# A fifth value chunk multiplied behind the arriving modulation, and modulation halves spread anew, in a two-layer float32 kernel

## The reference

```python
m_l = silu(c) @ ada_w + ada_b                       # six rows of 2048
n_l = rmsnorm(h_lat, g) * (1 + m_l[1]) + m_l[0]
z = gelu(n_l @ w_in); u, v = split(z, 2)            # w_in: 2048 x 8192
v = rmsnorm(v, g_v); s = einsum('gpq,bnqgc->bnpgc', w_s, v) + b_s
h_lat = h_lat + m_l[2] * ((u * s) @ w_out)          # w_out: 4096 x 2048
n_l = rmsnorm(h_lat, g2) * (1 + m_l[4]) + m_l[3]
h_lat = h_lat + m_l[5] * conv_ffn(n_l, ...)         # 2048 -> 11264 -> 2048
```

## Time and profile before

| | before |
|---|---|
| median of 3 runs | 2331.35 us (2327.18 to 2331.69) |
| profiled execution, its own time | 2325.37 us |
| its span, mean granted clock | 2323.7 us, 0.992 |
| TensorE products | 2277.0 us busy, 98% |
| VectorE, ScalarE, GpSimd | 1573.1, 1134.1, 113.5 us |
| loaded | 488.49 MB, 211 GB/s over the span |

### The profile page before, as it was taken

One profiled execution on the slowest core, in us unless ns is written; L12 is line 12 of the kernel. 1 busy time (PEld: TensorE's weight loads), 2 busy tenths in 40 slices (PEclk: granted clock), 3 DMA queues, 4 the chain that ended last, 5 costly groups with the idle time before them and its releaser, 6 DMA issues.

```text
span 2323.7 us, 34580 instructions
## 1 busy us (share of the span) xinstructions
PE 2277.0 (98%) x13320; PEld 1990.9 (86%) x13320; DVE 1573.1 (68%) x2103; ACT 1134.1 (49%) x1698; POOL 113.5 (5%) x206
## 2 busy tenths in 40 slices
PE   6999999999999999999999999999999999999998
PEld 5788888888888888888888889999999999878887
DVE  6988777677788865666656677566566645555655
ACT  3354444444454543555445564444544444555554
POOL 0010100011100100000000001000000000100000
PEclk9999999999999999999999999999999999999999
DMA  9999788789767765555555565444444545544453
GB/s 368 387 369 394 239 283 266 243 314 316 263 217 254 280 205 184 187 176 199 193 187 182 185 199 168 159 150 141 146 146 145 163 150 164 163 135 126 132 185 126
DMA packets 230043, 493.06 MB, mean 212 GB/s; under 512 B 9683, under 2 KB 12521, under 8 KB 226825
## 3 DMA queue, kind: packets, MB, share of 16 engines
q1 hardware_dynamic: 210384, 432.05, 55.1%
q0 software_dynamic: 14272, 50.99, 6.7%
q10 hardware_dynamic: 5256, 8.20, 1.1%
HBM read 488.49 MB, written 2.10 MB: 211 GB/s over the span
## 4 chain that ended last, share of the span: by engine, by line
PE 85%; DVE 6%; DMA 3%; issue 3%; ACT 1%; SPq 1%; POOL 0%; DVEq 0%; ACTq 0%; POOLq 0%
PE ps L1846 35%; PE ps L1893 22%; PE ps L1908 11%; PE ps L1910 5%; PE ps L2363 4%; DVE acc L1195 2%; DMA mods<-in_ada_w 2%; DVE wlo L1129 1%; PE ps L2186 1%; DMA ada<-in_ada_w 1%; SPq L414 1%; DVE acc L1138 1%; PE ps L2348 1%; PE ps L2205 1%; PE ps L2004 1%
## 5 line engine op out<-in xcount | busy, mean ns | idle before, releaser
L1129 DVE TENSOR_TENSOR wlo<-raw,whi 128x1024 fp32r<-128x1024 f32 x720 | 874.2, 1223 | 532.1 <-ACT whi L587 530.7
L587 ACT ACTIVATE whi<-raw 128x1024 fp32r<-128x1024 f32 x720 | 756.2, 1057 | 821.0 <-PE ps L1846 398.7
L1908 PE MATMUL ps<-xt__59,whi 128*128 128x512 f32 x1408 | 499.1, 399 | 5.8 <-DVE wlo L1129 4.3
L1910 PE MATMUL ps<-xt__59,wlo 128*128 128x256 f32 x1408 | 395.5, 281 | 0.0
L1846 PE MATMUL ps<-whi,xt__59 128*128 128x512 f32 x1024 | 329.7, 399 | 4.2 <-DVE xt__59 L1247 4.2
L1908 PEld LDWEIGHTS ps<-xt__59,whi 128*128 128x128 f32 x1408 | 265.3, 188 | 73.8 <-DVE wlo L1129 5.6
L1893 PE MATMUL ps<-xmh__60,whi 128*128 128x272 f32 x1088 | 322.7, 297 | 0.6 <-DVE h L1326 0.3
L1893 PE MATMUL ps<-xmh__60,wlo 128*128 128x272 f32 x1088 | 314.9, 289 | 0.0
L1893 PE MATMUL ps<-xml__61,whi 128*128 128x272 f32 x1088 | 313.0, 288 | 0.0
L1910 PEld LDWEIGHTS ps<-xt__59,wlo 128*128 128x128 f32 x1408 | 266.5, 189 | 0.1
L1846 PEld LDWEIGHTS ps<-whi,xt__59 128*128 128x128 f32 x1024 | 195.6, 191 | 46.1 <-issue 4.5
(11 more groups left out here) (335 smaller groups left out, 3267.8 us busy)
## 6 DMA issues: line engine op xcount, KB each, us to landing
raw<-in_a_w_in SPq DMA_DIRECT2D x128, 1024.0 KB, 5.5
raw<-in_ffn_w_up SPq DMA_DIRECT2D x88, 1024.0 KB, 5.1
ada<-in_ada_w POOLq DMA_DIRECT2D x96, 512.0 KB, 4.4
raw<-in_a_w_out SPq DMA_DIRECT2D x48, 1024.0 KB, 5.3
raw<-in_ffn_w_down SPq DMA_DIRECT2D x44, 1024.0 KB, 5.1
mods<-in_ada_w SPq DMA_DIRECT2D x64, 512.0 KB, 11.1
raw<-in_b_w_in SPq DMA_DIRECT2D x32, 1024.0 KB, 5.4
ada<-in_ada_w SPq DMA_DIRECT2D x16, 1024.0 KB, 8.9
```

The source lines that it names most:

```text
L587: act.activation(whi[:, r % 4], raw[:, r // 2, r % 2], ACT.Copy).then_inc(hi_ready, 1)
L1129: dve.tensor_tensor(wlo[:, r % 4], raw[:, r // 2, r % 2], whi[:, r % 4].bitcast(F32), ALU.subtract).then_inc(lo_ready, 1)
L1908: pe.matmul(both, whi[:, r % 4, i, c * P:c * P + P], xt_[:, :, k * T:k * T + T], start=first and i == 0, stop=last and i == 1, skip_group_ ...
L1910: mm = pe.matmul(ps[:, bank + c, 0:T], wlo[:, r % 4, i, c * P:c * P + P], xth[:, k, :], start=False, stop=last and i == 1, skip_group_chec ...
```

## The change

- Group g of the front has ten units for five v chunks (`S_ORDER`, `S_UNITS`): chunk 4 goes through banks 6 and 7 as well, behind chunk 3 in the same group. Each group has five slabs. Chunks 5 to 7 (24 units) are left for behind.
- ScalarE copies the parts of chunks 3 and 4 of groups 0 to 2 into three buffers each. VectorE adds them in group 3 (`add_parts`, `add_last`), the last part straight from PSUM. GpSimd's `add3` is gone.
- Six low parts instead of four stand between the additions of the next group. `keep_warm` has 8 transposes for 14.
- The memsets of `acc` on GpSimd wait until the last low tile is done (`nl` at 16), and `stream_ada(3)` until ten value outputs are.
- The 16 loads of `ada2` and their additions are spread over 12 slabs and 24 units, in place of 16 and 32.
- `ADA4_AT` has more in the first output chunk and fewer in the last, `ADA5_OUT_AT` eight for two, `ADA5_AT` six for eight in a pair.

```diff
-S_CHUNKS = (3, 0, 1, 2)
-LATE_LO = (0, 1, 2, 4)
+S_ORDER = ((3, 0, 4, 1, 2),) * 3 + ((3, 0, 1, 2, 4),)
+LATE_LO = (0, 1, 2, 4, 4, 5)
+S_UNITS = 10
...
 def first_unit(u):
...
-    g, i, half = u // 8, u % 8 // 2, u % 2
-    return S_CHUNKS[i], 4 * g + 2 * half
+    g, i, half = u // S_UNITS, u % S_UNITS // 2, u % 2
+    return S_ORDER[g][i], 4 * g + 2 * half
...
 def mod_adds(g, d):
...
-ADA4_AT = [(0, t) for t in (9, 11, 13, 15)] + [(n, t) for n in (1, 2) for t in (0, 4, 5, 6, 8, 9, 10, 12, 13, 14)]\
-    + [(3, t) for t in (0, 1, 2, 4, 5, 6, 7, 8)]
-ADA5_OUT_AT = (12, 13)
+ADA4_AT = [(0, t) for t in (6, 8, 9, 10, 11, 13, 14, 15)] + [(n, t) for n in (1, 2) for t in (0, 4, 5, 6, 8, 9, 10, 12, 13, 14)]\
+    + [(3, t) for t in (0, 4, 5, 6)]
+ADA5_OUT_AT = (7, 8, 9, 10, 11, 12, 13, 14)
...
-ADA5_AT = (0, 1, 2, 6, 8, 9, 10, 14)
+ADA5_AT = (0, 2, 6, 8, 10, 14)
...
-        whole3 = place("whole3", [P, 2, 512], O_H)
-        part3 = place("part3", [P, 2, 512], O_H + 4 * KB)
+        part3 = [place(f"part3{i}", [P, 2, 512], x) for i, x in enumerate((O_H, O_H + 4 * KB, O_H + 12 * KB))]
+        part4 = [place(f"part4{i}", [P, 2, 512], x) for i, x in enumerate((O_ADA, O_ADA + 4 * KB, O_H + 8 * KB))]
...
                     for i in range(2):
...
-                for q, c in enumerate(S_CHUNKS):
-                    slab(G_IN + g, q, w_in, g, c * 512 + GW)
-            for k in range(16):
-                slab(G_IN + 4 + k // 4, k % 4, w_in, k % 4, k // 4 * 512 + (4 * 512 + GW))
-                if k >= 4:
-                    sp.wait_ge(mod_added, mod_adds(3, 7) + k - 3)
-                else:
-                    sp.wait_ge(mod_added, mod_adds(3, last_in_slot(k)))
-                sp.dma_start(ada2[:, k % 4], ada_w[k * P:k * P + P, 2 * D:3 * D]).then_inc(mod_loaded[k % 4], 16)
+                for i, c in enumerate(S_ORDER[g]):
+                    n = 5 * g + i
+                    slab(G_IN + n // 4, n % 4, w_in, g, c * 512 + GW)
+            k = 0
+            for n in range(12):
+                slab(G_IN + 5 + n // 4, n % 4, w_in, n % 4, n // 4 * 512 + (5 * 512 + GW))
+                while k < 16 * (n + 1) // 12:
+                    if k >= 4:
+                        sp.wait_ge(mod_added, mod_adds(3, 7) + k - 3)
+                    elif last_in_slot(k) in PE_MOD[3]:
+                        sp.wait_ge(mod_turned, mod_columns(3))
+                    else:
+                        sp.wait_ge(mod_added, mod_adds(3, last_in_slot(k)))
+                    sp.dma_start(ada2[:, k % 4], ada_w[k * P:k * P + P, 2 * D:3 * D]).then_inc(mod_loaded[k % 4], 16)
+                    k += 1
...
-            def add3(g):
-                pool.wait_ge(sem("part3_copied"), 2 * g + 2)
-                if g > 1:
-                    pool.wait_ge(sem("part3_added"), g - 1)
-                pool.tensor_tensor(whole3[:, :, :], whole3[:, :, :], part3[:, :, :], ALU.add).then_inc(sem("part3_added"), 1)
-            add3(1)
-            add3(2)
...
+            pool.wait_ge(sem("nl"), 16)
...
-            add3(3)
+            pool.wait_ge(sem("v_ready"), 10)
...
-            stream_ada(5, 32, 0, 2)
+            stream_ada(5, 32, 0, 5)
...
-            stream_ada(5, 32, 2)
+            stream_ada(5, 32, 5)
...
-            def part3_out(g):
-                act.wait_ge(unit_used, 8 * g + 2)
-                if g > 1:
-                    act.wait_ge(sem("part3_added"), g - 1)
+            def part_out(g, part, used):
+                act.wait_ge(unit_used, used)
                 for tok in range(2):
-                    act.activation((part3 if g else whole3)[:, tok], ps[:, 6 + tok, :], ACT.Copy)\
-                       .then_inc(sem("part3_copied"), 1)
-            def v_out(c, par, used=None):
-                if par is None:
-                    act.wait_ge(sem("part3_added"), 3)
-                else:
+                    act.activation(part[g][:, tok], ps[:, 6 + tok, :], ACT.Copy).then_inc(sem("part_copied"), 1)
+            def v_out(c, par, used=None, whole=None, added=0):
+                if added:
+                    act.wait_ge(sem("part_added"), added)
+                if whole is None:
...
                 for tok in range(2):
-                    src = whole3[:, tok:tok + 1, :] if par is None else ps[:, 2 * par + tok:2 * par + tok + 1, :]
+                    src = ps[:, 2 * par + tok:2 * par + tok + 1, :] if whole is None else whole[:, tok:tok + 1, :]
...
                 for r in range(8):
                     if r == 3:
                         if first:
-                            v_out(2, 2, 32)
+                            v_out(3, 0, whole=part3[0], added=3)
...
-                    if first and r == 6:
-                        v_out(3, None)
+                    if first and r == 5:
+                        v_out(4, 0, whole=part4[0], added=6)
...
                     if first and r == 1:
-                        v_out(1, 1, 30)
+                        v_out(2, 2, 38)
...
             def ws_load(c):
...
             for g in range(4):
-                for u in (8 * g, 8 * g + 1):
+                for u in (10 * g, 10 * g + 1):
...
-                for i in range(8):
-                    u = 8 * g + i
+                for i in range(10):
+                    u = 10 * g + i
+                    if g == 3 and i == 9:
+                        v_out(0, 0, 34, added=5)
                     if i > 1:
...
-                    if i == 5:
-                        part3_out(g)
+                    if i == 5 and g < 3:
+                        part_out(g, part3, 10 * g + 2)
+                    if i == 9 and g < 3:
+                        part_out(g, part4, 10 * g + 6)
                     for k in (4 * g + 2 * i, 4 * g + 2 * i + 1) if i < 2 else ():
                         if k > 3:
...
-            v_out(0, 0, 28)
-            v_chunk(4, 0, True)
+            v_out(1, 1, 36)
+            v_chunk(5, 1, True)
...
-            v_chunk(5, 1)
...
                         for i in range(2):
...
-                    if g and d in LATE_LO:
-                        u = 8 * g - 4 + LATE_LO.index(d)
-                        lo(G_IN + u // 8, u % 8)
+                    for i, x in enumerate(LATE_LO):
+                        if g and d == x:
+                            u = S_UNITS * (g - 1) + 4 + i
+                            lo(G_IN + u // 8, u % 8)
...
+            def add_parts(part, n):
+                dve.wait_ge(sem("part_copied"), 12)
+                dve.tensor_tensor(part[0][:, :, :], part[0][:, :, :], part[1][:, :, :], ALU.add).then_inc(sem("part_added"), 1)
+                dve.wait_ge(sem("part_added"), n)
+                dve.tensor_tensor(part[0][:, :, :], part[0][:, :, :], part[2][:, :, :], ALU.add).then_inc(sem("part_added"), 1)
+            def add_last(part, n, used):
+                dve.wait_ge(unit_used, used)
+                dve.wait_ge(sem("part_added"), n - 1)
+                dve.tensor_tensor(part[0][:, :, :], part[0][:, :, :], ps[:, 6:8, :], ALU.add).then_inc(sem("part_added"), 1)
...
-                for u in (8 * g, 8 * g + 1):
+                for u in (S_UNITS * g, S_UNITS * g + 1):
...
-                for i in range(4 if g < 3 else 8):
-                    u = 8 * g + i
+                for i in range(4 if g < 3 else S_UNITS):
+                    u = S_UNITS * g + i
+                    if g == 3 and i == 4:
+                        add_parts(part3, 1)
+                        add_last(part3, 3, S_UNITS * 3 + 2)
+                    if g == 3 and i == 6:
+                        add_parts(part4, 4)
                     if i == 0:
...
-            for p in range(32):
-                lo(G_IN + 4 + p // 8, p % 8)
-                if p % 2:
-                    add2(p // 2)
+            k = 0
+            for p in range(24):
+                if p == 3:
+                    add_last(part4, 6, 40)
+                lo(G_IN + 5 + p // 8, p % 8)
+                while p >= 4 and k < 16 * (p - 3) // 20:
+                    add2(k)
+                    k += 1
...
-                    if n == 0 and t == 9:
+                    if n == 0 and t == 6:
...
                     if (n, t) in ADA4_AT:
...
-                    if n == 3 and t == 10:
+                    if n == 3 and t == 7:
...
                     if n == 3 and t in ADA5_OUT_AT:
...
                         if not (first and p == 0 and t < 4):
...
                         if p == 0 and first and t in ADA5_FIRST_AT:
-                            i = ADA5_FIRST_AT.index(t) + 2
+                            i = ADA5_FIRST_AT.index(t) + 8
...
                         if p == 0 and not first and t in ADA5_AT:
...
-                            ada_add(f * 4 + (31 + i // 2), f * 4 + (i // 2 - 1), i % 2, acc[:, 1])
+                            ada_add(f * 3 + (35 + i // 2), f * 3 + (3 + i // 2), i % 2, acc[:, 1])
...
             for g in range(4):
...
                 if g:
-                    keep_warm(6 + (g + 1) % 2, 14)
```

(19 more changed lines are left out.)

## The result

The changed kernel takes 2333.74 us (median of 20 runs, 2329.95 to 2338.44), the kernel before 2327.39 us beside it (20 runs). The ratio of the runs is 1.0025 with a 95% interval of 1.0019 to 1.0032: slower by 0.25%. The forecast was 4.4 us faster.

The account below looks back on a forecast made before the run. TensorE, busy 98% of the span, was taken as the bound, with VectorE's additions and their loads sharing the early part. Front +0.9, output product 0 and feed-forward -5.3 gave -4.4 us: 2331.35 to 2327.0, range 2319 to 2337.

Parts of the forecast that it names:

- The clock: Rival, chance 0.18: TensorE's clock falls at each group's start, 1.5 us each, three times 4.4; net 0, 2331.3 us.
- by the row they are not: Group starts: products at full clock right behind slow transposes mean keep-warm holds the clock, so not all three starts are slow.
- costs and gains nothing there: Group starts: keep_warm of 8 for 14 changes no time, since TensorE waits for the tiles either way.
- my 37.0: Front, groups 1 and 2: period of 36.8 us set by TensorE, plus 0.2 us for unit 7 coming late.
- my 40.5: Front, group 0: 36.8 us, plus 1.5 for its slow start and 2.2 of stall at units 6 and 7.
- The value chunks' stage: From group 3's start to the value chunks' end: 97.6 us, 5.1 over 92.5, with TensorE waiting for late low parts.
- The rival with 11 us: Chance 0.15: value-chunk weight loads take 11 us, not 7.9; 6.6 of queue plus 3.0 of clock, +5.2, 2336.6 us.
- What I set against the rival: Against the load queue making it slower: the queue is shorter now, since each load waits for an addition.
- the 57.8 us of VectorE on 51.7: Chunks 5 to 7: nineteen low parts and sixteen additions on VectorE against 19 TensorE units, over by 6.1 us.
- The forecast of +0.9 for the front: Value chunks end at 252.1 us against 251.2, group 3 starting at 154.5; bounds -6.8 and +5.3, more with the queue.
- the feed-forward: First part, four pairs: the new steps remove VectorE's late low parts, -5.3 us, bounds -3 and -5.8.
- The output product: More ADA4 and ADA5 additions, last chunk's lag inside VectorE's lead: charged 0, with 2 us as the upper end.

Follow-up runs that it names:

- Run 2: The changed kernel with keep_warm of 14 transposes again instead of 8: 2330.82 us, ratio 1.0013 to the kernel before.
- run 6: The changed kernel with keep_warm 14, transposes among the column products, in_ada_w loads one slab later and additions over 24 units: 2323.31 us, ratio 0.9983.
- Run 3: The changed kernel with each in_ada_w load for the third row one weight slab later in SP's queue: 2327.85 us, ratio 0.9998.
- run 4: Run 3's kernel with the sixteen in_ada_w additions spread over all 24 units behind group 3 instead of the last 20: 2326.04 us, ratio 0.9997.
- Run 7: Fewer ADA4 additions in the first output chunk: old front, new lists 2321.99 us; new front, keep_warm 14, run 4's edits 2320.46; that with last chunk thinned 2321.89.

## Why the prediction was wrong

**The clock, priced as a rival at 4.4 us and given 0.18.** It came true at all three starts, 0.76 us and a granted clock of 0.50 to 0.53. The step that failed is "by the row they are not": I read from one row at 104.8 that transposes keep the clock, though group 3 of the same kernel began at 0.77 behind as many, and forgot that the change itself takes six of fourteen away, which the forecast called a change that "costs and gains nothing there". Run 2 gives 2.9 us back, and in it the period of group 1 is 35.0 us and that of group 2 37.0, for my 37.0. Group 0 took 41.8 for my 40.5, with its slow stretch behind the columns 3 us rather than 1.7; in three of the nine traces with the new front it took 38.6 to 39.0. I had one value where there are two.

**The value chunks' stage: mis-sized, 97.6 for 105.9.** The chain was the one described: a weight load behind a modulation load that waits for an addition. Its first link was predicted for 46.8 us behind group 3's start and came at 51.5: issued 2.1 later, and 10.5 to land instead of 7.9. The rival with 11 us, given 0.15, was right on the first wait: ahead of unit 48 it had 3.3 us, and 3.38 were measured. It also said that such a gap may bring the lower clock, and it did (0.52 behind 211.5). It was wrong on the second, where it had another 3.3 on top of the forecast's 1.4: the wait ahead of unit 52 was 1.45. So 97.6, 6.6 of queue and the clock's 1.5 make 105.7 only by chance. The stage was 98.5 us busy and 7.4 idle, for 92.5 and 5.1 in the forecast: 2.3 us more of waiting and 6.0 more of busy time. Of the 6.0, some 3 are the lower clock (0.97 over 105.95 us), in two falls, at the start and behind the wait; 1.3 are a unit that costs more than 2.72 (93.8 busy for 34 units in run 6 at a clock of 1.00); what the rest is stays open. What I set against the rival, a queue shorter since each load waits, was wrong: the median to landing rose from 7.0 us (196 to 250 us, before) to 11.6. Run 3 takes 3.9 of the stage away; run 4 another 2.0 in its trace, which would fit the 57.8 us of VectorE on 51.7 but is within what the medians leave open.

**No case held both.** The forecast of +0.9 for the front with the clock's 4.4 and the queue's 6.6 makes 11.9; measured, 12.5. The sum is near, but its queue term is not what happened, as said above. I had treated as alternatives two mechanisms that do not exclude each other, so neither case reached it. That the measured time is inside the range (2319 to 2337) is luck: it took the feed-forward's 5.7, and a base that was 4.0 too high (2331.35 from 3 runs for 2327.39 from 20). From the assumed base the measured +6.35 would have given 2337.7.

**The output product: 0 taken, 2 as the upper end, 2.7 measured** (2.1 with the old front). I looked at the last chunk, and the loss was in the first, where eight additions in ten units ask for a half MB each and it lands 3.9 to 10.7 us after its issue, not always in the 4.4 of the page. TensorE's two gaps there are 2.1 of the 2.7. Run 7 shows that the last chunk was the next in line.

**Right:** the feed-forward, -5.7 for -5.3, with the mechanism (no gap in the four pairs; 181.0 to 182.4 in the eleven kernels with the new lists, gaps of 1.1 us at most); the parts added by VectorE in group 3 without a gap; the memsets beside them, charged at nothing (at 162.81 one of 1.84 us beside additions of 1.22 and 1.23); the place of group 0's stalls (units 6 and 7, 0.29 and 1.05 us for the 2.2 predicted).

**Open:** why TensorE's clock falls behind the column products in some executions of the same instructions and not in others, and so what decides between a group 0 of 38.7 and of 41.8 us. Open too: whether it is the number of transposes ahead of a group or the shorter gap behind them that holds the clock.

## What to carry to other kernels

When loads that wait for a consumer share a queue with loads that feed the critical engine, put the waiting one behind, not ahead: here one slab's place in a queue was worth 3.9 us in the traces of the stage, while the landing time itself got longer. Rivals that do not exclude each other need a case of their own with their prices added. Small work that looks idle, like six transposes, may be holding a clock: price its removal by what the rows show with and without it. And when a sum of terms comes out right, compare each term, busy and idle apart: here 105.7 met 105.9 with a queue term that was far too large.

## What the hardware showed that was not expected

- Eight transposes (1.07 us) ahead of a group and then a gap of 0.99 us: a first product of 0.76 or 0.77 us in twelve of fifteen starts, and a fall within 3 us in two more. Fourteen (1.73 us) and a gap of 0.33: 0.47 us in twelve of twelve.
- Group 0 of the new front took 38.6 to 39.0 us in three traces and 40.3 to 42.3 in the other six. The nine differ in transposes at most, and four have the very same instructions there: 38.6, 38.7, 41.8 and 41.8.
- A wait of 3.38 us in the middle of the value chunks was followed by a granted clock of 0.52 for 3.1 us, and one of 4.49 in the output product by a product of 0.79 us. One of 2.10 in run 3 was followed by a product of 0.50.
- With both kinds of 1 MB loads in one queue and the DMA at 375 to 385 GB/s, a slab took 11.6 us to land; asked for earlier, 14.3, and the kernel was faster.
